# A two-layer hybrid decoder trunk: turning sliding attention's operands on VectorE instead of TensorE, differential queries normed in one piece, the residual loaded in four parts

## What is computed

```python
def hybrid_layer(x, norm_g, w_in, w_out, ...):
    h = rms_norm(x, norm_g)
    p = jnp.einsum('btd,dp->btp', h, w_in)
    (aq, ak, av, alr, az, bq, bk, bv, bz, cq, ck, cv, cz, dqkv, dbeta, da, dz) = jnp.split(p, offs, axis=-1)
    ya = gla_mixer(aq, ak, av, alr, gla_w_lr2, gla_b_lr2, gla_norm_g) * jax.nn.silu(az)
    yb = swa_mixer(bq, bk, bv, swa_q_norm_g, swa_k_norm_g, swa_sinks, slopes_b) * jax.nn.silu(bz)
    yc = diff_mixer(cq, ck, cv, diff_q_norm_g, diff_k_norm_g, diff_lambda, diff_subln_g, slopes_c,
                    lambda_init) * jax.nn.silu(cz)
    yd = gdn_mixer(dqkv, dbeta, da, gdn_conv_w, gdn_A_log, gdn_dt_bias, gdn_norm_g) * jax.nn.silu(dz)
    y = jnp.concatenate([ya, yb, yc, yd], axis=-1)
    return x + jnp.einsum('btm,md->btd', y, w_out)

# in swa_mixer: q and k are normed per head, the scores are masked to a window of 128
    q = rms_norm(q..., q_g); k = rms_norm(k..., k_g)
    s = jnp.einsum('bgrnid,bgnjd->bgrnij', q, kb) * d ** -0.5
# in diff_mixer: q and k are normed per head and half (64 wide)
    q = rms_norm(q..., q_g) * dq ** -0.5; k = rms_norm(k..., k_g)
```

## Time and profile before

| | us |
|---|---|
| median of 3 runs | 1786.48 (1784.94 to 1787.24) |
| the profiled execution | 1785.59 |
| its span, first to last instruction | 1783.8 |
| PE busy in it | 1776.5 (100%) |
| DVE busy | 1049.8 (59%) |
| ACT busy | 496.7 (28%) |
| POOL busy | 920.0 (52%) |

### The profile page before, as it was taken

One profiled execution on the slowest core, in us unless ns is written; L12 is line 12 of the kernel. 1 busy time (PEld: TensorE's weight loads), 2 busy tenths in 40 slices (PEclk: granted clock), 3 DMA queues, 4 the chain that ended last, 5 costly groups with the idle time before them and its releaser, 6 DMA issues.

```text
span 1783.8 us, 23623 instructions
## 1 busy us (share of the span) xinstructions
PE 1776.5 (100%) x9126; PEld 1457.3 (82%) x9126; DVE 1049.8 (59%) x2393; ACT 496.7 (28%) x945; POOL 920.0 (52%) x864
## 2 busy tenths in 40 slices
PE   9999999999999999999999999999999999999999
PEld 7788888888888887788887888888888878877887
DVE  7776877834433674544656779778444337755342
ACT  6213123122222543322312131231322224433220
POOL 5556545545555444445565555454455454444454
PEclk9999999999999999999999999999999999999999
DMA  7556545545555667445765566455555556674556
GB/s 273 177 189 212 183 149 167 188 144 185 174 183 175 203 196 253 148 159 179 255 233 168 189 200 200 144 168 169 163 185 176 168 180 204 196 257 142 166 168 209
DMA packets 108336, 333.40 MB, mean 187 GB/s; under 512 B 11680, under 2 KB 24512, under 8 KB 107968
## 3 DMA queue, kind: packets, MB, share of 16 engines
q1 hardware_dynamic: 43904, 155.73, 26.6%
q0 software_dynamic: 40320, 146.82, 26.1%
q10 hardware_dynamic: 24000, 29.34, 4.8%
HBM read 319.25 MB, written 12.60 MB: 186 GB/s over the span
## 4 chain that ended last, share of the span: by engine, by line
PE 94%; DMA 2%; DVE 2%; ACT 1%; POOL 0%; issue 0%; SPq 0%; ACTq 0%; POOLq 0%
PE acc L566 84%; PE mix L608 3%; DMA w_hi<-in_wstream 1%; PE mix L841 1%; DMA w_raw<-in_wstream 1%; PE mix L771 1%; PE mix L861 1%; PE mix L796 1%; DMA slots<-in_x 0%; POOL w_lo L523 0%; PE mix L748 0%; PE mix L967 0%; PE mix L948 0%; PE mix L874 0%; PE mix L852 0%; DVE actT_lo L1518 0%
## 5 line engine op out<-in xcount | busy, mean ns | idle before, releaser
L523 POOL TENSOR_TENSOR w_lo<-w_raw,w_hi 128x512 fp32r<-128x512 f32 x575 | 760.0, 1324 | 605.1 <-DMA w_hi<-in_wstream 461.6
L566 PE MATMUL acc<-w_hi,actT_hi 128*128 128x512 f32 x1408 | 558.2, 396 | 0.1
L566 PE MATMUL acc<-w_hi,actT_lo 128*128 128x512 f32 x1408 | 548.6, 390 | 0.0
L566 PE MATMUL acc<-w_lo,actT_hi 128*128 128x512 f32 x1408 | 548.4, 389 | 0.0
L566 PE MATMUL acc<-actT_hi,w_hi 128*128 128x512 f32 x896 | 357.4, 399 | 1.2 <-issue 0.8
L566 PE MATMUL acc<-actT_hi,w_lo 128*128 128x512 f32 x896 | 349.5, 390 | 0.0
L566 PE MATMUL acc<-actT_lo,w_hi 128*128 128x512 f32 x896 | 349.1, 390 | 0.0
L566 PEld LDWEIGHTS acc<-w_hi,actT_hi 128*128 128x128 f32 x1408 | 264.5, 188 | 56.1 <-issue 2.8
L566 PEld LDWEIGHTS acc<-w_hi,actT_lo 128*128 128x128 f32 x1408 | 264.3, 188 | 55.6
L566 PEld LDWEIGHTS acc<-w_lo,actT_hi 128*128 128x128 f32 x1408 | 264.6, 188 | 52.1
L494 POOL DMA_DIRECT2D w_hi<-in_wstream x280 | 159.2, 568 | 246.2 <-PE acc L566 234.6
(11 more groups left out here) (267 smaller groups left out, 1626.0 us busy)
## 6 DMA issues: line engine op xcount, KB each, us to landing
w_raw<-in_wstream SPq DMA_DIRECT2D x288, 512.0 KB, 4.1
w_hi<-in_wstream POOLq DMA_DIRECT2D x280, 512.0 KB, 3.8
out_x<-slots ACTq DMA_DIRECT2D x7, 1024.0 KB, 8.3
slots<-in_x ACTq DMA_DIRECT2D x1, 4096.0 KB, 19.8
slots<-out_x ACTq DMA_DIRECT2D x1, 4096.0 KB, 20.1
slots<-in_x SPq DMA_DIRECT2D x3, 1024.0 KB, 11.7
slots<-rows ACTq DMA_DIRECT2D x2, 1024.0 KB, 7.2
hops<-smT ACTq DMA_DIRECT2D x16, 128.0 KB, 3.2
```

Source lines behind the costliest of these rows:

```text
L523: pool.tensor_tensor(w_lo[:, n % RING], w_raw[:, g % RAW, k], w_hi[:, g % HI, k].bitcast(F32), ALU.subtract).then_inc(w_ready, 1)
L566: last = nc.tensor.matmul(acc[b][:, :], lhsT, rhs, start=(k == 0 and i == 0), stop=(k == kts - 1 and i == 2))
```

## The change

1. **SWA's q and k.** The six transposes a tile on PE (`tr`, 24 a layer) go. During the GLA tiles ACT squares bq and bkv whole, DVE sums them, norms them in one piece and turns them by 32x32 blocks straight into `QT` (slot 8, 16 instructions of 32x512) and `KT` (slot 6, 16 of 32x256) (`swa_queries`, `swa_keys`). ACT scales `QT` in place by the product of both norm weights. bq moves from slot 8 to 11.
2. **SWA's outputs.** DVE turns the gated outputs bz into slot 8 (`turn_bz`): 16 instructions of 32x128 for a tile, within tile t those of tile t-1, half ahead of `den` and half behind `normalise`; all 16 of tile 3 at the end. `turn_y` for bz goes from PE, and `y_hi`, `y_lo` read slot 8.
3. **Differential q.** Squared by ACT after chunk cq, normed by DVE in one piece and turned by 4 instructions into slot 7 (that of av) after the last GLA tile, copied to `hops` by one DMA of 1 MB from ACT's queue (`hop_q_out`), for which DVE waits before SWA's first bias, since that writes slot 7. In the SWA tiles only ck is normed and turned, both pieces over `smT`.
4. **Residual.** Four DMAs of 1 MB: the first where the one was, the others at the start of differential tiles 3, 2 and 1; DVE waits for each by itself.
5. **Begin.** `first_tile` issues kt 0's twelve matmuls by term and not by accumulator; weight pair 0 comes in two DMAs; ACT squares x kt 0 only after it has split kt 1; x kts 4 to 7 come in two DMAs; the squares are added later; `x_sums` stands behind the last kt of dq and not ahead of it; parameter, constant and `ws` loads are issued later.
6. All four block rows of dz are turned after GLA tile 0 (they were spread over tiles 0 and 1).

```diff
-SLOT = dict(dq=4, ..., bq=8, bkv=9, ...)
+SLOT = dict(dq=4, ..., bq=11, bkv=9, ...)
+QT_SLOT = 8
...
             x_in(0)
-            weights(0)
+            sp.dma_start(w_raw[:, 0, 0], wstream[0][:, 0:GW]).then_inc(first_raw_in, 16)
+            sp.dma_start(w_raw[:, 0, 1], wstream[0][:, GW:2 * GW]).then_inc(raw_in[0], 16)
             x_in(1)
...
-                pe.wait_ge(N_DVE.sem, N_DVE.at(l, f"{t}.bk"))
-                for h in H:
-                    nc.tensor.transpose(mh[0][:, h], q[:, t, h * HD:h * HD + HD], ident)
-                for g in range(2):
-                    last = nc.tensor.transpose(mh[1][:, g], kv[:, t, g * HD:g * HD + HD], ident)
-                last.then_inc(B_PE.sem, B_PE.one(f"{t}.tr"))
                 yield
-                pe.wait_ge(B_ACT.sem, B_ACT.at(l, f"{t}.kT"))
-                if t:
+                if t == 0:
+                    pe.wait_ge(G_ACT.sem, G_ACT.at(l, f"gq{HEADS-1}"))
+                    pe.wait_ge(G_DVE.sem, G_DVE.at(l, "tk"))
+                else:
                     pe.wait_ge(B_DVE.sem, B_DVE.at(l, f"{t-1}.y3"))
...
-                    if k == KT - 1:
-                        x_sums(l)
                 project(l, 0, 0, KT, 0, turned=True, ahead=h_ready)
+                x_sums(l)
...
-                            if k == 2:
-                                for m in range(2 * HEADS, 3 * HEADS):
-                                    turn_y(l, m)
...
+                    if CHUNKS[8 + t] == "bq":
+                        for m in T:
+                            nc.scalar.activation(W["QT"][:, m], slot(SLOT["bq"])[:, m], ACT.Square)
+                    if CHUNKS[8 + t] == "ck":
+                        act.wait_ge(G_DVE.sem, G_DVE.at(l, "tc"))
+                        act.dma_start(hops[l, 0], slot(SLOT["av"])).then_inc(hop_q_out, 16)
...
-                act.dma_start(xT, (out if l else x).rearrange("(k p) n -> p k n", p=P)).then_inc(xres_in, 16)
+                def residual(n):
+                    k = slice(4 * n, 4 * n + 4)
+                    act.dma_start(xT[:, k], (out if l else x).rearrange("(k p) n -> p k n", p=P)[:, k]) \
+                        .then_inc(xres_in[n], 16)
+                residual(0)
...
+                def swa_queries():
+                    dve.wait_ge(G_ACT.sem, G_ACT.at(l, "rq"))
+                    q = slot(SLOT["bq"]).rearrange("p t (h c) -> p (t h) c", h=HEADS)
+                    dve.tensor_tensor(q, q, cols(rsb_q), ALU.mult).then_inc(G_DVE.sem, G_DVE.one("nq"))
+                    for r in range(P // BLK):
+                        for f in range(P // BLK):
+                            last = dve.transpose(dst[fs, :, :, rs_], src[rs_, :, :, fs])
+                def turn_bz(t, rows):
+                    dve.wait_ge(B_DVE.sem, B_DVE.at(l, f"{t}.y3"))
+                    for r in rows:
+                        for f in range(P // BLK):
+                            last = dve.transpose(dst[fs, :, rs_], src[rs_, :, fs])
...
+                    if t == 0:
+                        dve.wait_ge(hop_q_out, 16 * (l + 1))
```

296 lines of the change are left out of this document (199 added, 97 removed).

## The result

| us | before | changed |
|---|---|---|
| median | 1786.51 (1784.94 to 1787.24, 4 runs) | 1773.65 (1773.30 to 1774.03, 4 runs) |
| the profiled execution | 1785.59 | 1773.94 |
| its span | 1783.8 | 1772.1 |

The ratio is 0.9929 (95% interval 0.9912 to 0.9946): 0.7% faster.

What follows compares the result with a forecast made beforehand. PE's own instruction stream bounds the kernel from 12.6 us on. Span: -5.28 - 3.50 - 0.39 + 0.10 + 0 = -9.07 us, to 1774.7; plus 1.8 and 0.9 gives 1777.4 us, range 1774.5 to 1781.5.

Steps and rivals of the forecast that it cites:

- Part 1: SWA tiles: the six q and k transposes a tile leave PE, 0.11 us each, -5.28 us in two layers.
- Part 2: First output chunk: bz's sixteen transposes a layer leave PE, 1.75 us for each layer, -3.50 us.
- Part 5: Work moved to DVE and ACT, checked place by place: 0 us, as long as the leads over PE hold.
- (a): GLA tiles: DVE's added norm, turns and sum fit its idle gaps, behind tile 1 ending 1 to 4 us early.
- (b): SWA tiles: tightest is tile 2; 5.54 us leave DVE, 5.32 us of bz's turns come in, some 2.9 us stay free.
- part 3: Sum of squares moved behind dq: 0.39 us wait goes, 0.05 us lost in each layer on dk's lead; -0.3 us.
- part 4: The very start: earlier first matmul and later square of kt 0 cancel; 0 us, bounds -0.7 and +0.4.
- (c): Last SWA tile and first output chunk: bz's last turns end in time, the chain behind PE's transposes shortens; priced within 0 us.
- A lead that runs out: Rival: DVE ends 1 to 2 us late in GLA tile 1 or SWA tile 2; 1779.4 to 1781.4 us, chance 0.07.
- Slower through bz's turns: Rival, SWA tiles: each 32x128 turn costs 0.725 us, PE waits 9.1 us a layer; 1795.6 us, chance 0.03.
- The copy late: Rival: differential query copy lands at 603, PE waits some 3.4 us a layer before SWA; 1784.2 us, chance 0.04.
- Duration as cost: Rival: each of 80 removed PE transposes costs its 0.273 us duration, 21.8 us instead of 8.8; 1764.4 us, chance 0.02.

Runs made afterwards that it cites:

- the dummies: Changed kernel with unread PE transposes of a constant added: six at each SWA tile's head, 1779.65 us; separately, sixteen in each layer's first output chunk, 1777.89 us.
- two pairs of kernels: Kernel before with the new beginning alone against before: ratio 0.9991; changed kernel (1773.55 us) against the changed kernel with the old beginning (1776.33 us).
- after_queries_turned_twice: Changed kernel with DVE's sixteen turns of SWA's queries done a second time behind GLA tile 1: 1789.3 us, ratio 1.0020.

## Why the prediction missed, step by step

**What bounds the kernel: right.** A dense pace of 65.51 us for 288 matmuls in both profiles, and every microsecond of transposes taken out is a microsecond of span. The transposes are 8.8 us of the 11.65 by which the span fell.

**Part 1, right:** -5.28 forecast, -5.32 in the profile, 5.34 put back by the dummies. **Part 2, right in its price:** -3.50 forecast, 3.52 put back. The profile shows 4.17 for the stage; the other 0.65 us were waits of the kernel before that the forecast didn't count as its own. **Part 5, right that the leads hold:** no wait of PE came from DVE's or ACT's new work. (a) Behind GLA tile 1 DVE is idle for 4.4 us, a little over the 1 to 4 forecast (the lead itself is 6.0), since sixteen turns took 11.45 and the norm 2.29 us. (b) SWA tile 2 keeps 0.69 us at the outputs and 1.67 us at the next bias. (d) The copy is issued at 581.28 and lands in 5.2 us, 7.5 us ahead. (e) As said.

**The step that failed is the price of PE's waits in the kernel before.** The forecast took PE's own time right and let the waits stand: it counted 0.39 us of them as gone (part 3, 0.29 net of a price) and put the rest at nothing, or in the range alone. Between the two profiles PE's waits fell from 4.0 to 1.8 us, and 2.8 us went besides the transposes' 8.8. The terms that were too small:

- *Parts 3 and 4, the beginning:* -0.3 and 0 forecast, 1.2 us in the first two profiles (1.1 in layer 1, 0.1 in layer 2), 1.7 and 2.8 in the medians of two pairs of kernels, some 2 on average. In the two profiles 0.65 us of the 1.1 are gained up to the start of kt 14, which is part 4's matter, and 0.44 behind it, which is part 3's forecast almost to the number. But other executions of kernels with the old order wait 0.2 to 1.5 us at the sum, a size that one profile can't tell. And part 4 judged the start by the chain to kt 2 alone (in the changed kernel kt 2 starts at 12.08 instead of 12.60 us), while other executions of the old order wait at kt 4. The diff also moves three loads of constants on ACT's and SP's queues, and the forecast never priced them. ACT's 5.05 us without work before its fifth weight pair stand in the trace of before and were the row to look for.
- *Part 5 (c), the first output chunk:* the forecast says that this chain becomes shorter and prices it at 0. It was worth 0.65 us between the two profiles and 0.8 on average.
- *The wait in a GLA tile* stood in the range alone, as one that may not recur. It recurs in every profile of the old tiles; the change took 0.44 us of it, and why is open: no run separates what the change moves in the GLA tiles.

**The conversion from span to median** made the miss larger. I added the 0.9 us by which the kernel before's median was over its profiled execution. That difference was scatter: in the repeat of before both are 1785.29, and the medians of before lie between 1785.29 and 1786.78 from one set of runs to another. The changed kernel's median is 0.3 us *under* its profiled execution. That is 1.2 of the 3.75 us by which the forecast is high; the rest is 2.6 us of span: 0.9 in the beginnings of both layers, 0.7 in the first output chunk, 0.8 in dz (chance) and ck, 0.2 in small steps. The range had 2.7 us below the forecast for a better start, the GLA wait and the scatter between runs; all three were used up, and the output chunk came on top.

**The part 3 price for dk's lead** (0.1 us lost) didn't show: dk has no wait in any profile with the sums behind dq.

**The rivals.** A lead that runs out: none did, and after_queries_turned_twice shows what it would cost. Slower through bz's turns: a turn took 0.31 us, not 0.64 or more. The copy late: no. Duration as cost: refuted by the dummies.

## What to carry to other kernels

A small wait of the bounding engine in one profile marks a place where two chains meet; its size in that execution isn't the worth of removing it. A second profile of the unchanged kernel costs little and shows which waits recur; the range should reach to what the chain costs when it comes late. Loads that nobody needs yet, issued while the first weights come in, are not free: find who idles for a transfer in the first 30 us. When PE will stand still for some microseconds (2.7 and 5.4 here), count the slower clock behind it too. And when an operand moves from PSUM to SBUF, the operations that read it next should be placed clear of GpSimd's two-source work.
